# Attention steps on TensorE: a step's probability transposes ahead of the scores two steps on

## What is computed

```
s = q @ k.T (+ bias, neighbourhood heads, latent queries only)
p = softmax(s, axis=-1)          # 128 queries x 128 or 384 keys
o = p @ v
out = concat(o over heads) @ w_out
```

## Time and profile before

| | before |
|---|---|
| median of three runs | 1612.38 us |
| the profiled execution, its own time | 1616.16 us |
| its span, first to last instruction | 1614.4 us |
| TensorE busy | 1548.5 us (96%) |
| VectorE busy | 1011.2 us (63%) |
| ScalarE busy | 576.1 us (36%) |
| mean granted TensorE clock | 0.978 of full speed |
| attention loop, T(0) to T(22) | 433.82 to 484.95 us |

### The profile page before, as it was taken

One profiled execution on the slowest core, in us unless ns is written; L12 is line 12 of the kernel. 1 busy time (PEld: TensorE's weight loads), 2 busy tenths in 40 slices (PEclk: granted clock), 3 DMA queues, 4 the chain that ended last, 5 costly groups with the idle time before them and its releaser, 6 DMA issues.

```text
span 1614.4 us, 23466 instructions
## 1 busy us (share of the span) xinstructions
PE 1548.5 (96%) x9279; PEld 1515.8 (94%) x9279; DVE 1011.2 (63%) x1254; ACT 576.1 (36%) x704; POOL 102.2 (6%) x55
## 2 busy tenths in 40 slices
PE   7889999989889899999989999998999999999999
PEld 7889999989759899999989999998999989999999
DVE  5776767858886667667857676785754344334323
ACT  3322322254483533232253332226434235323321
POOL 3120000026201000000010000001000010000000
PEclk9999999989999899999989999998999999999999
DMA  9345455634214355546525554563623322333332
GB/s 369 134 194 195 172 180 213 241 113 173 89 53 147 131 182 191 199 166 224 209 105 202 188 187 180 203 237 131 224 90 131 131 104 105 123 130 111 133 128 91
DMA packets 49641, 262.64 MB, mean 163 GB/s; under 512 B 6704, under 2 KB 7984, under 8 KB 27568
## 3 DMA queue, kind: packets, MB, share of 16 engines
q1 hardware_dynamic: 49584, 261.85, 45.0%
HBM read 259.60 MB, written 2.23 MB: 162 GB/s over the span
## 4 chain that ended last, share of the span: by engine, by line
PE 79%; issue 8%; DVE 6%; DMA 3%; ACT 2%; POOL 1%; SPq 1%; POOLq 0%; DVEq 0%; ACTq 0%
PE ps L1023 16%; PE ps L1024 16%; PE ps L1026 16%; PE ps L997 8%; PE ps L999 8%; PE ps L998 8%; DMA raw<-panels 3%; DVE mprod L670 2%; DVE w_lo L662 1%; PE ps L1082 1%; ACT w_hi L456 1%; PE ps L1193 1%; PE ps L1036 1%; PE ps L1039 1%; PE ps L1037 1%
## 5 line engine op out<-in xcount | busy, mean ns | idle before, releaser
L662 DVE TENSOR_TENSOR w_lo<-raw,w_hi 128x2048 fp32r<-128x2048 f32 x164 | 380.4, 2319 | 282.6 <-ACT w_hi L456 282.3
L1023 PE MATMUL ps<-x_hi,w_hi 128*128 128x384 f32 x1536 | 523.0, 341 | 18.3 <-ACT x_hi L486 7.1
L1024 PE MATMUL ps<-x_hi,w_lo 128*128 128x384 f32 x1536 | 521.5, 340 | 0.0
L1026 PE MATMUL ps<-x_lo,w_hi 128*128 128x384 f32 x1536 | 518.9, 339 | 0.0
L456 ACT ACTIVATE w_hi<-raw 128x2048 fp32r<-128x2048 f32 x169 | 323.0, 1911 | 321.8 <-PE ps L999 153.8
L670 DVE SCALAR_TENSOR_TENSOR mprod<-mraw,cB 128x1024 f32<-128x1024 f32 x256 | 315.4, 1232 | 7.3
L1023 PEld LDWEIGHTS ps<-x_hi,w_hi 128*128 128x128 f32 x1536 | 293.3, 191 | 22.9 <-issue 10.5
L1024 PEld LDWEIGHTS ps<-x_hi,w_lo 128*128 128x128 f32 x1536 | 293.2, 191 | 0.0
L1026 PEld LDWEIGHTS ps<-x_lo,w_hi 128*128 128x128 f32 x1536 | 292.7, 191 | 0.0
L997 PE MATMUL ps<-act_hi,w_hi 128*128 (+1 forms) x832 | 279.8, 336 | 1.3 <-DVE w_lo L662 1.3
L999 PE MATMUL ps<-act_hi,w_lo 128*128 (+1 forms) x832 | 279.6, 336 | 0.0
(11 more groups left out here) (130 smaller groups left out, 1110.4 us busy)
## 6 DMA issues: line engine op xcount, KB each, us to landing
raw<-panels SPq DMA_DIRECT2D x169, 1024.0 KB, 4.8
mraw<-mod_rows SPq DMA_DIRECT2D x128, 512.0 KB, 3.6
mshift<-mod_rows SPq DMA_DIRECT2D x8, 512.0 KB, 14.5
mscale<-mod_scale SPq DMA_DIRECT2D x6, 512.0 KB, 12.2
bias<-na_bias SPq DMA_DIRECT2D x1, 2048.0 KB, 8.1
h<-x_in_t SPq DMA_DIRECT2D x1, 1536.0 KB, 7.0
out<-h SPq DMA_DIRECT2D x4, 384.0 KB, 2.3
cB<-cond_rows SPq DMA_DIRECT2D x1, 1024.0 KB, 9.0
```

Of the source, the lines that this page charges most:

```text
L662: nc.vector.tensor_tensor(w_lo[q0 % 2][:, :], raw[q0 % 2][:, :], w_hi[q0 % 2][:, :].bitcast(F32), ALU.subtract).then_inc(lo_done, 1)
L1023: mm(out, hi[:, cols], x_hi[:, k, :], start=(k == 0), stop=False)
L1024: mm(out, lo[:, cols], x_hi[:, k, :], start=False, stop=False)
L1026: last = mm(out, hi[:, cols], x_lo[:, k, :], start=False, stop=(k == KD - 1))
```

## The change

In the loop of TensorE, the call for T(i) now stands ahead of the call for S(i + 2) instead of behind it. Nothing else differs: the same instructions, operands, waits and banks, and the orders of the other engines are as before. S(i + 2) keeps its wait for exp(i), T(i) its waits for norm(i) and pT(i - 1).

```
             for i in range(STEPS - 1):
+                p_transposes(i)
                 if i + 2 < STEPS:
                     scores(i + 2)
-                p_transposes(i)
                 for j in TR_LATE.get(i, ()):
                     pe.wait_ge(tr_act, j - 1)
                     transposed(j)
```

## The result

The changed kernel took 1650.14 us (median of four runs, 1647.45 to 1652.81) against 1612.36 us before. The ratio is 1.0237 with a 95% interval of 1.0216 to 1.0258: 37.8 us or 2.4% slower. The forecast was 1643.0 us, with a range of 1634 to 1656.

The account below looks back on a forecast made before the run. The loop was taken as nearly full on TensorE and VectorE at once, through their overlap. Losing it costs 25.1 us, low clock 5.5, together 30.6 on the 1612.4 us median: 1643.0 us, range 1634 to 1656.

Parts of the forecast that it names:

- ring: Attention loop: norm(i) on VectorE, T(i) and S(i + 2) on TensorE, then top(i + 2), without overlap; 25.1 us longer.
- six turns: Start-to-start passes, three per pair: 3.31, 3.56 and 4.14 us with bias, 3.31, 2.84 and 3.42 without.
- the walk of 76.3: Loop from T(0) to T(22), start-to-start times added up at full clock: 76.3 us.
- The panel split: VectorE work between norm(6) and top(8): 2.21 us, of which TensorE's 1.35 us hide part, so it costs 0.86.
- The covers: V, exponentials, copy pT and `o_lo` in the loop cost nothing, being hidden; margin 3 us on either side.
- turn B: From top of kind 2 through norm and T to S of kind 0: 4.14 us with bias, 3.42 without.
- The clock: TensorE's granted clock in the loop: drops to 1.2 GHz after long idle times, 5.5 us in all.
- turn C: From top of kind 0 through norm and T to S of kinds 1: 3.31 us.
- four dips: Low-clock spells after TensorE's four idle times clearly longer than 1.70 us, each 1.37 us: 5.5 us.
- Rival 2: TensorE's low clock through the whole loop: 56 us more, 1668 us; chance 0.08.
- Rivals 3 and 4: Loop: scores hidden anyway, 1612 us, chance 0.04; late T and its copy start earlier, 1606.8 us, chance 0.02.
- Rival 5: Loop slows by half the size, one term running beside another: 1618 to 1634 us; chance 0.03.

Follow-up runs that it names:

- the filled kernel: Changed kernel plus constant, unused matmuls in TensorE's idle time, five per turn that V does not fill and ten ahead of T(0): 1639.15 us.
- the first profile: Profiled execution of the changed kernel, no further edit: 1647.45 us own time, T(0) to T(22) in 85.5 us at a clock of 0.78.
- the second profile: Changed kernel run again without edit: 1652.59 us, T(0) to T(22) in 90.0 us at a clock of 0.72.
- the normalisation with 15 fillers: Kernel before plus unused constant matmuls in five normalisations, 15 ahead of the spreading matmul and 13 behind it: 1613.25 us, ratio 0.9995.
- 6 and 5: Kernel before plus unused constant matmuls in five normalisations, 6 ahead of the spreading matmul and 5 behind it: 1605.38 us, ratio 0.9949.

## Why the prediction was right, and which term was off

- **The order of waits.** It said that VectorE's queue makes a ring of the change, since top(i + 2) stands behind norm(i) there and S(i + 2) now behind T(i). Shown: 37.8 us of waiting for scores where 3.3 us stood, and losses that add over the halves of the loop. The prediction gave the wait of before as 1.5 us, which leaves out the 1.8 ahead of the bias add; no term of its sum hangs on that.
- **The terms.** All six turns came within 0.05 us of their sums, and the filled kernel's loop within 2.8 us of the walk of 76.3. The panel split, priced at 0.86, cost 0.73 there at full clock (455.45 to 459.79, 4.34 us for a turn of 3.61).
- **The covers.** The exponentials, the copy and `o_lo` stayed hidden when all turns were changed. V stayed hidden at full clock. At the low level it did not: T(4) started at 451.23, 0.3 us after its product had ended at 449.96 + 0.96, and T(13), T(16) and T(22) 0.5 to 0.7 us after theirs. That is the second of the prediction's own signs of being wrong, V ending after norm in turn B; it costs some 2 us of the 9.3 below.
- **The clock.** This is the term that was mis-sized. The mechanism was named, its price for a turn was right (turn C from 438.85 to 443.56 in the profile after, 4.71 us for 3.31, so 1.40 where the prediction had 1.37), and its count was too low. I charged four dips, 5.5 us, by picking the idle times clearly longer than the 1.70 us ahead of the one dip of before. Measured were 9.3 us above the walk in the first profile and 13.7 in the second, with 38 and 50 us at the low level instead of the 12 that four dips like that of before make. My upper bound of one dip for each pair, 11 us, was exceeded too in the second profile, and by the medians (37.8 - 25.1 = 12.7), though not in the first profile.
- **What the count rested on.** Two readings of it were wrong. The 18 waits for the product in the earlier trace rows, 0.85 us each, of which "one alone was followed by a dip", are waits of the weight loads. The matmuls of TensorE stood idle for the product only 6 times before, 4.3 us in all, and the longest of these, 1.70 us, is the one that the dip followed; ahead of it only one other idle time in the loop, 1.50 us for a copy (448.59), was as long as 1.5. So the trace of before held almost no evidence that such idle times are harmless. And the change makes an idle time that was not counted: T(0) now stands ahead of S(2), and TensorE idles 1.94 us before it where it idled 0.28. The clock fell right there in the first profile. The 2.80 us of the first turn B, in turn, are only 1.4 to 2.1, since the late transposes fill part of it. With the idle time ahead of T(0) as a fifth dip the charge would have been 5 x 1.37 = 6.9 us instead of 5.5, still short of 9.3. Which of the idle times inside the loop bring the low clock, no run here tells, since they were filled together.
- **Rival 2**, the low clock all through with 56 us, was half right: the clock of the loop was 0.72 to 0.81 in three profiles and not 0.5, and it cost 8.9 to 13.7 us and not 31. Transposes at 0.87 us behind an idle time of 1.59, at 454.31 in the profile after, speak against the strong form of the rule that was weighed there, by which they would run at the low level, as the row of before did. No run here tells whether a transpose counts for less than a matmul.
- **Rivals 3 and 4** (scores hidden anyway, late T moved forward) fell, with every single turn 9 to 10 us slower. Rival 5, a ring of half the size, fell with the filled kernel, whose ring costs 26.6 us.
- **The sum** of 30.6 us stands against 37.8 measured; 25.1 for the ring (26.6 in the filled kernel) and the rest, as far as the profiles show it (9.3 and 13.7), clock. That the time lies in the range is in part luck: 1650.1 is above 1612.4 + 36.1 = 1648.5, the bound with the most dips that I had allowed, and only the margins of 3 us for the covers and 3.8 us for the profiled execution, neither meant for the clock, took the range up to 1656.

## What to carry to other kernels

In an engine's queue, an instruction that is early for everyone may be put ahead of one that waits, but not the other way round: whatever stands behind the wait takes on all of the wait's conditions, and if the other engine's queue orders the same two items the other way, overlap turns into a ring. A ring is easily priced: add the start-to-start times once round, per kind of turn, and check that what you call hidden fits into the idle time of its own engine. Price the clock in the same step: where the new order makes TensorE idle in every turn, count low clock for a good part of the stretch (here 37.6 of 85.5 us and 50.4 of 90.0), not for its longest idle times alone. And when you look for idle times that did no harm, read those of the matmuls, not the waits of the weight loads, which run beside earlier matmuls (4.3 us against 15.3 in the loop of before).

## What the runs showed of the hardware that I had not expected

- The granted clock stayed at its lower level for 20 us on end although TensorE was busy 16.1 of 20.6 us there. In the profiled loop of before it fell once only. In the normalisation with 15 fillers it fell while TensorE had no idle time at all.
- Work whose result nobody uses made the changed kernel 13.4 us faster, and the kernel before 9 us faster, by making the stretches of low clock shorter. The amount matters: a constant 128 x 128 float32 matmul took 6.49 / 15 = 0.43 us, nearly all of it at the low level (3.06 / 13 = 0.24 at the full one), so 15 of them outlasted the gap of 2.6 us and gave back the gain, while 6 and 5 kept it.
- Executions of one and the same program differed by 2 to 12 us, the slower ones mostly at a lower granted clock (1657.11 us at 0.963 against 1645.05 at 0.970); the changed kernel's loop alone took 85.2, 85.5 and 90.0 us in three profiles.
